# Reordering three waits in a two-layer streaming encoder step

## The chip, the cores and the metric

The kernel runs on one core of one Trainium2 chip, as one program. The metric is the device time of an execution in microseconds. An execution's profile has its own span, from the first to the last instruction, a little under its time.

## The reference

One inference step of two layers over 1074 columns: 16 meta tokens, 1024 prompt tokens, 32 sample tokens and 2 columns of padding, each with 1024 features.

```python
z = rmsnorm(x, norm_mix_g) @ w_in                 # split: c_q 768, c_kv 256, k_r 32, x_r 512, g_r 512
q = rmsnorm(c_q, q_norm_g) @ w_uq                 # 8 heads of 64 + 32 rotary
ckv, kpe = rmsnorm(c_kv, kv_norm_g), rope(k_r)
xc = causal_conv4(x_r); r, i = sigmoid(blockdiag(xc)), sigmoid(blockdiag(xc))
h = scan(a*h + sqrt(1-a^2)*(i*xc)); y = h * gelu(g_r)
k, v = ckv_keys @ w_ukv                           # K 64 and V 64 per head
o = softmax(mask(q k / sqrt(96))) v               # chunk-causal, chunks of 64
h = x + concat(rmsnorm(o), rmsnorm(y)) @ w_out
x = h + square(relu(rmsnorm(h) @ w_up)) @ w_down  # 4096 wide
```

After the second layer follows a last RMSNorm. All is float32.

## The kernel before

Activations lie transposed: 128 features on the partitions, the tokens along a row. Weights come in blocks of 128x1024, one DMA each from SyncE into `raw`. ScalarE rounds a block into `whi`, VectorE subtracts to get the remainder `wlo` (`split(b)` on either engine), and TensorE makes each product in three passes (high x high, high x low, low x high) over the k-steps, a pass being three matmuls of some 358 columns (`product`, L947 to L960). The results of one product fill three PSUM banks, banks 0 to 2 and 3 to 5 in turn (a slot); a product therefore waits (`take`) until the results of the product two before it have been read. Banks 6 and 7 take sums of squares and the first head's maxima.

There is no scheduler. Each engine's instructions stand in the order of its own function, and semaphores with counted values tie them together. A wait holds all that stands behind it on its engine. The places of the change are:

The start of a layer. In the first layer products 0 and 1 of the x_r columns are interleaved. In the second, product `U_XR[0]` is followed by `mix_sum` (L993), a product of a matrix of ones with `msq`, the sum of the squared inputs; its result goes into the root that scales every output of the input projection. VectorE builds `msq` by seven additions (`next_sq`, `next_sum`, L3098 to L3103), at the end of the first layer's `closing`, beside the last additions of the MLP (`d_sum`), the low parts of the next inputs (`next_low`) and the split of the first two weight blocks (`next_split`).

The maxima of the first head (`max_step(0, s)`, L1088). For each head the row maximum of the masked scores is needed as a shift for the exponentials. It is taken over 11 steps, `MAXES`. TensorE writes a step's scores into one of two banks, alternately (`max_bank`), and VectorE's `reduce_max(h, s)` takes the maxima of its parts; step s waits for the reduction of step s - 2, `w("mxred", h * NMX + s - 1)`. For head 0 the steps stand between the four K products (`B_UK`, three banks of 432 columns each) and the ten V tiles (six matmuls of 512 columns each, L1132 to L1145). `max_rows` (L1119) then transposes the maxima on TensorE, ScalarE copies them out (`shift_hi`, behind the copy of V tile 5), VectorE makes the low part (`shift_lo`), and SyncE and GpSimd write both into rows of the query tile (`qe`) by DMA (`few_shifts` for GpSimd); attention starts when all of them have landed. Behind reduction 3, VectorE also makes `kslot_lo`, a subtraction of 33x1296 with two inputs in SBUF, while GpSimd does three such subtractions (`low_parts`).

The output projection. Eight products of the LRU half (`U_OY`), then eight of the attention half (`U_OO`). VectorE adds the first eight to x (`add_y(i)`, an addition of one slot), normalises the last pair of heads (`divide(3)`, which waits until GpSimd's DMAs have spread the inverted sums of the softmax), and makes the low parts of the attention output (`o_low`). Product i of the LRU half waits for `add_y(i - 2)`. ScalarE's stream is the counterpart: high parts, squares, roots.

The MLP that follows takes about half of the time. It multiplies by blocks of two-level combinations of the weights (seven products in place of eight); its weight buffers are filled by DMAs that SyncE and GpSimd issue when the split of their last content is done.

Of the kernel before, what the change touches and what calls it, by code (L numbers as in the profile page):

```python
# [356 lines left out]
NMX = len(MAXES)  # L357
# [60 lines left out]
def trunk(nc, xT, wst, vec, fgain, ropeC, ropeS, ident_in, past_ckv, past_kpe, h0, conv0,  # L418
          yT, ckv_out, kpe_out, h_out, conv_out, x_scr, sum_scr):
    ctx = ExitStack()  # L420
    with ctx:
# [498 lines left out]
        def _(pe):  # L920
# [5 lines left out]
            for L in range(DEPTH):  # L926
# [20 lines left out]
                def product(dst, u, b, woff, rhs_h, rhs_l, ready=None):  # L947

                    w("w_lo", b + 2)
                    take(u)  # L950
                    n = len(rhs_h)
                    for k in range(n):
                        if ready:
                            ready(k)
                        for i, (a, c) in enumerate(PASSES):
                            wt = (whi if a == "h" else wlo)[b % 2][:, woff + 128 * k:woff + 128 * k + 128]
                            r = (rhs_h if c == "h" else rhs_l)[k]
                            for q in range(3):
                                mm = nc.tensor.matmul(dst(q), wt, r(q), start=(k == 0 and i == 0), stop=(k == n - 1 and i == 2))  # L959
                    mm.then_inc(S["mm"], 1)  # L960
# [32 lines left out]
                def mix_sum():  # L993

                    if L:
                        pe.wait_ge(S["sq_sum"], L * 7 + 7)
                        sum_of_squares(SUM_MIX, msq)
                    else:
                        w("sum_lo", SUM_MIX)
                        sum_of_parts(SUM_MIX, rs_r, msq_r)  # L1000
# [10 lines left out]
                if L == 0:  # L1011

                    for k, c in [(0, 0), (1, 0), (0, 1), (1, 1)] + [(k, c) for k in range(2, 8) for c in (0, 1)]:
                        dst = to_slot(U_XR[c])
                        for i, (a, b) in enumerate(PASSES):
                            if k == 0 and i == 0:
                                w("w_hi", B_XR[c] + 1)
                            if k == 0 and i == 2:
                                w("w_lo", B_XR[c] + 2)
                            if c == 0 and i == 0:  # L1020
                                w("xg_hi", k + 1)
                            if c == 0 and i == 1:
                                w("xg_lo", k + 1)
                            wt = (whi if a == "h" else wlo)[B_XR[c] % 2][:, 128 * k:128 * k + 128]
                            for q in range(3):
                                mm = nc.tensor.matmul(dst(q), wt, (XH if b == "h" else XL)[k](q), start=(k == 0 and i == 0), stop=(k == 7 and i == 2))  # L1026
                        if k == 7:
                            mm.then_inc(S["mm"], 1)
                    mix_sum()
                else:  # L1030
                    product(to_slot(U_XR[0]), U_XR[0], B_XR[0], 0, XH, XL, x_ready)
                    mix_sum()
                    product(to_slot(U_XR[1]), U_XR[1], B_XR[1], 0, XH, XL)

                XHL, XLL = [tok(t, LIVE) for t in xgh], [tok(t, LIVE) for t in xgl]

# [87 lines left out]
                for j in range(4):  # L1124
                    product(lambda q: ps[:, 3 * slot_of(U_K + j) + q, 0:KCH], U_K + j, B_UK, 256 * j,
                            [(lambda q, t=t: t[:, q * KCH:(q + 1) * KCH]) for t in ckvh],
                            [(lambda q, t=t: t[:, q * KCH:(q + 1) * KCH]) for t in ckvl])
                    if j >= 1:
                        max_step(0, 2 * j - 2)
                        max_step(0, 2 * j - 1)  # L1130
                w("w_lo", B_UV + 2)
                for t in range(10):  # L1132
                    if t < 3:
                        w("kf", 3)
                    else:
                        w("v_ev", t - 2)
                    c0 = VTILES[t]
                    for k in range(2):
                        for i, (a, c) in enumerate((("h", "h"), ("h", "l"), ("l", "h"))):
                            mm = nc.tensor.matmul(ps[:, 3 + t % 3, :], (ckvh if a == "h" else ckvl)[k][:, c0:c0 + P],  # L1140
                                                  (whi if c == "h" else wlo)[B_UV % 2][:, 512 * k:512 * k + 512],
                                                  start=(k == 0 and i == 0), stop=(k == 1 and i == 2))
                    mm.then_inc(S["mm"], 1)
                    if t + 6 < NMX:
                        max_step(0, t + 6)  # L1145
                    if t == 5:
                        max_rows(0)

                w("kf", 4)
# [992 lines left out]
        def _(dve):  # L2142
# [34 lines left out]
            for L in range(DEPTH):  # L2177
# [448 lines left out]
                o_low(2)  # L2626
                add_y(1)
                split(31)
                divide(3)
                add_y(2)  # L2630
                o_low(3)
                split(32)
                add_y(3)
                sum_lo(osq_r, osq, osqt_r, SUM_O)
                add_y(4)
                split(33)
# [417 lines left out]
                def closing():  # L3054

                    j = NPAIR - 1

                    def at(name, k):
                        dve.wait_ge(S[name], L * PER[name] + pairs(name, j) + k)

                    last_third_sum()
                    up_block_sum(NGROUP, 0, 2)
                    up_lo(j, 3)
                    up_lo(j, 4)
                    c_sum(at, 0)
                    up_lo(j, 5)
                    relu(at, 0, False)
                    up_lo(j, 6)
                    up_lo(j, 7)
                    c_sum(at, 1)  # L3070
                    relu(at, 1, False)
                    up_lo(j, 8)
                    f_low(at, 0)
                    c_sum(at, 2)
                    relu(at, 2, False)
                    f_low(at, 1)
                    up_lo(j, 9)
                    relu(at, 3, False)
                    f_low(at, 2)
                    up_lo(j, 10)  # L3080
                    d_sum(at, j, 0)
                    f_low(at, 3)
                    for n in range(1, 4 if L < DEPTH - 1 else 6):
                        d_sum(at, j, n)
                    if L < DEPTH - 1:

                        def next_low(m):

                            dve.wait_ge(S["xg_hi"], L * 8 + 8 + (m + 1))
                            at("d_add", DONE_AT[m])  # L3090
                            lo(xgl[m][:, :], x[m], xgh[m][:, :], "xg_lo", col(V_GNEXT + m))

                        def next_split(b):

                            dve.wait_ge(S["w_hi"], (L + 1) * B_MLP + b + 1)
                            V.tensor_tensor(wlo[b][:, :], raw[b][:, :], whi[b][:, :].bitcast(F32), ALU.subtract).then_inc(S["w_lo"], 1)

                        def next_sum(m):  # L3098

                            dve.wait_ge(S["sq"], L * 8 + 8 + m + 1)  # L3100
                            if m > 1:
                                dve.wait_ge(S["sq_sum"], L * 7 + 7 + m - 1)
                            V.tensor_tensor(msq[:, :], msq[:, :], next_sq[m][:, :], ALU.add).then_inc(S["sq_sum"], 1)  # L3103

                        for n in range(4, 16):
                            d_sum(at, j, n)
                            if n in (5, 7, 8, 10, 12, 14):
                                next_low((5, 7, 8, 10, 12, 14).index(n))
                            if n in (9, 13):
                                next_sum((n - 5) // 4)  # L3110
                            if n == 11:
                                next_split(0)
                        next_low(6)
                        next_sum(3)
                        next_low(7)
                        for m in (4, 5, 6, 7):
                            next_sum(m)
                        next_split(1)
                    else:
                        for n in range(6, 24):  # L3120
                            d_sum(at, j, n)
                            if n in (15, 17, 19, 20, 22):
                                end_scale(0, (15, 17, 19, 20, 22).index(n))
                        for m in range(5, 8):
                            end_scale(0, m)
                        for q in (1, 2):
                            for m in range(8):
                                end_scale(q, m)
# [343 lines left out]
```

## Time and profile before

| what | us |
|---|---|
| three timed runs | 2481.19, 2485.27, 2485.93 |
| median | 2485.27 |
| profiled execution, its own time | 2481.51 |
| its span | 2479.70 |

The timeline view lists instructions by start time, with neighbours of the same kind merged (x3 is three of them), their time together, and in brackets the idle time in front with what ended it, if there was any to speak of. TensorE's matmuls overlap in it: each lasts until its result is out, while the next one starts when its columns have been fed, so for TensorE it is the distance of the starts that counts. Its durations are modelled.

### The profile page before, as it was taken

The numbers are of one execution on the slowest core, as the hardware profiler recorded it, in microseconds if no ns is written. First come the engines' busy times: TensorE is split into PE (matmuls) and PEld (weight loads), VectorE is DVE, ScalarE is ACT, GpSimd is POOL, SyncE is SP. The second block draws the span as 40 slices with busy tenths as digits, with TensorE's granted clock in tenths as the row PEclk, the third lists the DMA queues.
The fourth block names the chain that finished last, engine by engine and source line by source line (L and its number), as shares of the span: only waits on it lengthen the run. The fifth ranks groups of instructions, "written<-read, shape, count | busy, mean of one in ns | idle before, by whom it ended". The sixth has DMA issues, their size and how long they took to land.

```text
span 2479.7 us, 43928 instructions
## 1 busy us (share of the span) xinstructions
PE 2458.4 (99%) x17424; PEld 2371.6 (96%) x17424; DVE 1802.2 (73%) x2778; ACT 1220.1 (49%) x2197; POOL 516.0 (21%) x478
## 2 busy tenths in 40 slices
PE   9999999999999999999999999999999999999998
PEld 9999977899999999999999999779999999999997
DVE  7678766579776777677676797674887766776676
ACT  5455355535554454454524653555355544554455
POOL 0024155200112211221201232541001112111222
PEclk9999999999999999999999999999999999999999
DMA  4122201213347635764731222012135467546655
GB/s 155 59 60 72 61 11 38 84 57 110 87 93 137 121 86 102 132 116 89 220 99 52 61 72 61 11 38 89 60 114 99 92 122 130 104 91 117 130 113 172
DMA packets 104537, 230.39 MB, mean 93 GB/s; under 512 B 14816, under 2 KB 17984, under 8 KB 104336
## 3 DMA queue, kind: packets, MB, share of 16 engines
q0 software_dynamic: 43648, 89.14, 20.9%
q1 hardware_dynamic: 60544, 138.42, 17.7%
q8 instruction: 139, 2.28, 0.4%
q14 instruction: 62, 0.51, 0.1%
q10 hardware_dynamic: 144, 0.04, 0.0%
HBM read 144.03 MB, written 81.18 MB: 91 GB/s over the span
## 4 chain that ended last, share of the span: by engine, by line
PE 91%; DVE 4%; DMA 2%; issue 2%; ACT 1%; POOL 0%; SPq 0%; DVEq 0%; ACTq 0%; POOLq 0%
PE ps L959 27%; PE ps L1304 23%; PE ps L1353 20%; PE ps L1168 5%; PE ps L1183 4%; PE ps L1445 2%; PE ps L1238 2%; PE ps L1115 2%; PE ps L1416 1%; DMA raw_all<-in_wst 1%; PE ps L1026 1%; PE ps L1140 1%; PE ps L1047 1%; DVE wlo L2809 1%; DVE raw_all L2941 0%
## 5 line engine op out<-in xcount | busy, mean ns | idle before, releaser
L1974 ACT ACTIVATE whi<-raw_all 128x512 fp32r<-128x512 f32 (+1 forms) x420 | 250.2, 600 | 348.2 <-DVE raw_all L2941 128.0
L2809 DVE TENSOR_TENSOR wlo<-raw_all,whi 128x512 fp32r<-128x512 f32 (+1 forms) x420 | 271.4, 652 | 174.6 <-ACT whi L1974 170.5
L3307 POOL DMA_DIRECT2D x_scratch<-stage x224 | 199.7, 942 | 845.9 <-DVE stage L2951 698.1
L2027 ACT ACTIVATE stage<-ps 128x536 f32<-128x536 f32 (+1 forms) x224 | 135.3, 610 | 110.0 <-PE ps L1353 104.6
L1497 ACT ACTIVATE whi<-raw_all 128x1024 fp32r<-128x1024 f32 (+3 forms) x72 | 66.7, 926 | 236.9 <-PE ps L959 234.4
L2951 DVE TENSOR_TENSOR stage<-stage,ps 128x536 f32<-128x536 f32 (+1 forms) x168 | 118.8, 707 | 85.8 <-PE ps L1353 84.8
L2519 DVE TENSOR_REDUCE mxp<-ps 64x1 f32<-64x64 f32 (+11 forms) x384 | 140.3, 372 | 55.0 <-PE ps L1115 48.4
L959 PE MATMUL ps<-xgh,whi 128*128 128x358 f32 (+1 forms) x720 | 157.3, 327 | 0.0
L959 PE MATMUL ps<-xgl,whi 128*128 128x358 f32 (+1 forms) x720 | 156.6, 325 | 0.0
L959 PE MATMUL ps<-xgh,wlo 128*128 128x358 f32 (+1 forms) x720 | 156.5, 325 | 0.0
L959 PEld LDWEIGHTS ps<-xgl,whi 128*128 128x128 f32 x720 | 124.0, 189 | 0.0
L959 PEld LDWEIGHTS ps<-xgh,whi 128*128 128x128 f32 x720 | 123.4, 189 | 0.5 <-issue 0.2
L959 PEld LDWEIGHTS ps<-xgh,wlo 128*128 128x128 f32 x720 | 123.3, 189 | 0.0
L2194 DVE TENSOR_TENSOR wlo<-raw_all,whi 128x1024 fp32r<-128x1024 f32 (+3 forms) x70 | 87.3, 1247 | 40.9 <-ACT whi L1497 40.5
L1168 PE MATMUL ps<-pn,v 128*65 128x320 f32 (+1 forms) x288 | 106.3, 452 | 0.0
L1755 ACT ACTIVATE pn<-ps 128x320 f32<-128x320 f32 (+1 forms) x144 | 65.4, 454 | 71.4 <-PE ps L1183 70.0
L2941 DVE TENSOR_TENSOR raw_all<-raw_all 128x256 f32<-128x256 f32 x224 | 90.4, 419 | 11.6 <-DMA raw_all<-in_wst 10.5
L1183 PE MATMUL ps<-qo,koh 128*128 128x320 f32 (+7 forms) x304 | 97.0, 400 | 0.0
L1183 PE MATMUL ps<-qe,keh 97*128 97x320 f32 (+7 forms) x304 | 95.7, 396 | 0.9 <-DMA qe<-mt 0.7
L1755 ACT ACTIVATE pd<-ps 16x64 f32<-16x64 f32 (+4 forms) x352 | 56.8, 224 | 55.5 <-PE ps L1183 55.2
L3292 POOL DMA_DIRECT2D raw_all<-in_wst x30 | 29.8, 993 | 254.8 <-DMA raw_all<-in_wst 254.8
L1183 PEld LDWEIGHTS ps<-qe,keh 97*128 97x128 f32 x304 | 54.6, 190 | 26.5 <-issue 7.4
(835 smaller groups left out, 7680.0 us busy)
## 6 DMA issues: line engine op xcount, KB each, us to landing
raw_all<-in_wst SPq DMA_DIRECT2D x232, 256.0 KB, 3.3
raw_all<-in_wst SPq DMA_DIRECT2D x80, 512.0 KB, 3.6
x_scratch<-stage POOLq DMA_DIRECT2D x112, 268.0 KB, 5.8
x_scratch<-stage POOLq DMA_DIRECT2D x112, 264.0 KB, 5.8
x_scratch<-xall POOLq DMA_DIRECT2D x24, 537.0 KB, 3.6
xall<-x_scratch SPq DMA_DIRECT2D x24, 537.0 KB, 9.4
xall<-in_xT SPq DMA_DIRECT2D x16, 537.0 KB, 7.4
raw_all<-in_wst POOLq DMA_DIRECT2D x30, 256.0 KB, 4.0
```

The costliest lines, as they stand in the source:

```text
L959: mm = nc.tensor.matmul(dst(q), wt, r(q), start=(k == 0 and i == 0), stop=(k == n - 1 and i == 2))
L1168: mm = nc.tensor.matmul(ps[0:65, bank, c0:c0 + n], v[:, v0:v0 + 65], p_tile(gk)[:, 0:n], start=(k in FIRST), stop=(k in LAST))
L1183: mm = nc.tensor.matmul(ps[:, gi % 3, 0:n], ks[e][0 if a == "h" else 1][rows, k0:k0 + P], qs[e][0 if c == "h" else 1][rows, q0:q0 + n], st ...
L1304: mm = nc.tensor.matmul(ps[:, 2 * slot_ + t, 0:HN], wt, rhs[:, t * HN:(t + 1) * HN], start=(opens and n == 0), stop=(n == 11), skip_group_ ...
L1353: mm = nc.tensor.matmul(ps[:, 2 * slot_ + t, 0:HN], ring(u, whi if a == "h" else wlo)[:, wc], fop[q, f + c][:, t * HN:(t + 1) * HN], start ...
L1755: ins = nc.scalar.activation(dst[r0:r1, c0:c1], src[r0:r1, c0:c1], ACT.Exp, scale=SM_SCALE)
L1974: nc.scalar.activation(dst, src, ACT.Copy).then_inc(S["u_hi"], 1)
L2027: nc.scalar.activation(quarters(stage_of(L, g, i, n)[:, 0:N2]), src, ACT.Copy, scale=-1.0 if row else 1.0).then_inc(S["x_copy"], 1)
L2519: ins = V.reduce_max(mxp[lo_:hi_, tile, part:part + 1], ps[lo_:hi_, max_bank(h, s), c0:c0 + n], AX_X)
L2809: V.tensor_tensor(dst, src, hi.bitcast(F32), ALU.subtract).then_inc(S["u_lo"], 1)
L2951: V.tensor_tensor(st, st, src, op).then_inc(S["x_add"], 1)
L3307: pool.dma_start(x_scr[2 * i + row, :, a:b], stage_of(L, g, i, n)[:, 0:b - a], accum_op=ALU.add).then_inc(S[done], 16)
```

## The change

Four edits in the order of instructions. The computation is the same, and so is the number of instructions of each engine.

1. On TensorE, in the second layer, `mix_sum` stands inside product `U_XR[1]`, ahead of its k-step 2, and not ahead of the whole product.
2. On VectorE, at the end of the first layer, `next_split(1)` (the low part of the weights of that product) stands ahead of the last four `next_sum`, not behind them.
3. On TensorE, head 0's steps stand in threes (0 to 2, 3 to 5, 6 to 8) behind K products 1 to 3, and steps 9 and 10 behind V tiles 0 and 1; before there were pairs, and one step behind each of V tiles 0 to 4. The transposition stands behind V tile 3, not 5. This holds for both layers.
4. On VectorE, `add_y(2)` stands ahead of `divide(3)`, and `add_y(3)` right behind it, ahead of `o_low(3)` and `split(32)`.

```diff
                     product(to_slot(U_XR[0]), U_XR[0], B_XR[0], 0, XH, XL, x_ready)
-                    mix_sum()
-                    product(to_slot(U_XR[1]), U_XR[1], B_XR[1], 0, XH, XL)
+                    product(to_slot(U_XR[1]), U_XR[1], B_XR[1], 0, XH, XL, lambda k: mix_sum() if k == 2 else None)
...
                     if j >= 1:
-                        max_step(0, 2 * j - 2)
-                        max_step(0, 2 * j - 1)
+                        for s in range(3 * j - 3, 3 * j):
+                            max_step(0, s)
...
-                    if t + 6 < NMX:
-                        max_step(0, t + 6)
-                    if t == 5:
+                    if t + 9 < NMX:
+                        max_step(0, t + 9)
+                    if t == 3:
                         max_rows(0)
...
                 add_y(1)
                 split(31)
+                add_y(2)
                 divide(3)
-                add_y(2)
+                add_y(3)
                 o_low(3)
                 split(32)
-                add_y(3)
                 sum_lo(osq_r, osq, osqt_r, SUM_O)
...
                         next_low(7)
+                        next_split(1)
                         for m in (4, 5, 6, 7):
                             next_sum(m)
-                        next_split(1)
```

TensorE's order of the first layer between K products 1 and 3, before. `keh` holds the first head's keys and `qe` its queries, and a row with them is a part of a step; the rows of L959 are the K product between the two pairs of steps.

```order
L1115 MATMUL ps<-keh,qe 128x144 [waits kslot_hi,k_hi,root,q_hi,qn_hi]
L1115 MATMUL ps<-keh,qe 128x272
L1115 MATMUL ps<-keh,qe 128x16
L1115 MATMUL ps<-keh,qe 128x400
L959 MATMUL ps<-ckvh_111,whi_51 128x432 [waits kf,w_lo]
...
L959 MATMUL ps<-ckvh_112,wlo_53 128x432 x3
L1115 MATMUL ps<-keh,qe 128x400 [waits mxred]
L1115 MATMUL ps<-keh,qe 128x128 [waits mxred]
L1115 MATMUL ps<-keh,qe 128x176
```

And of the changed kernel, in the same place.

```order
L1114 MATMUL ps<-keh,qe 128x144 [waits kslot_hi,k_hi,root,q_hi,qn_hi]
L1114 MATMUL ps<-keh,qe 128x272
L1114 MATMUL ps<-keh,qe 128x16
L1114 MATMUL ps<-keh,qe 128x400
L1114 MATMUL ps<-keh,qe 128x400 [waits mxred]
L959 MATMUL ps<-ckvh_111,whi_51 128x432 [waits kf,w_lo]
...
L1114 MATMUL ps<-keh,qe 128x128 [waits mxred]
L1114 MATMUL ps<-keh,qe 128x176
L1114 MATMUL ps<-keh,qe 128x512 [waits mxred]
L1114 MATMUL ps<-keh,qe 128x144 [waits mxred]
L1114 MATMUL ps<-keh,qe 128x272
```

Step 2 (400 columns, waiting for a reduction) now stands directly behind steps 0 and 1 and ahead of the K product, and the next group has steps 3, 4 and 5.

VectorE's order in the first layer's output projection, before. `o_150` is the last pair of heads, L2608 is `add_y`, and x_in7 and x_in0 name the additions with number 2 and 3.

```order
L2194 TENSOR_TENSOR wlo_53<-raw_all,whi_51 128x1024 [waits w_hi]
L2552 MEMSET o_150 128x2 [waits o_ev,inv_in]
L2553 TENSOR_TENSOR o_150<-o_150,rc 128x1072
L2608 TENSOR_TENSOR xall<-xall,ps 128x1074 [waits mm,x_in7]
L2224 SCALAR_TENSOR_TENSOR ol_166<-o_150,vecs,oh_162 128x1074 [waits o_sq,o_hi]
L2194 TENSOR_TENSOR wlo_52<-raw_all,whi_50 128x512 [waits w_hi]
L2608 TENSOR_TENSOR xall<-xall,ps 128x1074 [waits mm,x_in0]
```

And of the changed kernel, where each line number is one less.

```order
L2193 TENSOR_TENSOR wlo_53<-raw_all,whi_51 128x1024 [waits w_hi]
L2607 TENSOR_TENSOR xall<-xall,ps 128x1074 [waits mm,x_in7]
L2551 MEMSET o_150 128x2 [waits o_ev,inv_in]
L2552 TENSOR_TENSOR o_150<-o_150,rc 128x1072
L2607 TENSOR_TENSOR xall<-xall,ps 128x1074 [waits mm,x_in0]
L2223 SCALAR_TENSOR_TENSOR ol_166<-o_150,vecs,oh_162 128x1074 [waits o_sq,o_hi]
L2193 TENSOR_TENSOR wlo_52<-raw_all,whi_50 128x512 [waits w_hi]
```

Each of the two additions has moved up: the first past the division and its wait for `inv_in`, the second past a low part and a split.

## Rows read from the trace of the kernel before

**Rows 1.** The page, busy us and share of each engine.
```profile
PE 2458.4 (99%) x17424; PEld 2371.6 (96%) x17424; DVE 1802.2 (73%) x2778; ACT 1220.1 (49%) x2197; POOL 516.0 (21%) x478
```

**Rows 2.** Timeline, TensorE: start, us, instruction, count, idle before; first layer's output projection.
```profile
487.39 0.66 PE L959 MATMUL ps<-yh,wlo 128*128 128x358 f32 x3
489.05 0.72 PE L959 MATMUL ps<-yh,whi 128*128 128x358 f32 x3 [1.01 <-DVE xall L2608]
...
494.51 0.66 PE L959 MATMUL ps<-yh,wlo 128*128 128x358 f32 x3
495.18 0.73 PE L959 MATMUL ps<-yh,whi 128*128 128x358 f32 x3
```

**Rows 3.** Timeline, VectorE, the same stretch.
```profile
486.45 1.27 DVE L2553 TENSOR_TENSOR o<-o,rc 128x1072 f32<-128x1072 f32 x1 [7.65 <-issue]
...
487.64 1.26 DVE L2608 TENSOR_TENSOR xall<-xall,ps 128x1074 f32<-128x1074 f32 x1
```

**Rows 4.** The chain that ended last: start, us, what; second layer's output projection.
```profile
1698.43 34.87 PE ps L959 x216
```

**Rows 5.** Timeline, TensorE, start of the second layer.
```profile
1254.21 0.65 PE L959 MATMUL ps<-xgh,wlo 128*128 128x358 f32 x3
1255.46 2.14 PE L976 MATMUL ps<-msq,ones 128*128 128x512 f32 x6 [0.61 <-DVE msq L3103]
```

**Rows 6.** Timeline, VectorE and ScalarE, start of the second layer.
```profile
1249.99 5.41 DVE L3103 TENSOR_TENSOR msq<-msq,next_sq 128x1074 f32<-128x1074 f32 x4
1255.32 1.22 DVE L3096 TENSOR_TENSOR wlo<-raw_all,whi 128x1024 fp32r<-128x1024 f32 x1
...
1263.17 1.12 ACT L1559 ACTIVATE rs<-ps,eps 128x1024 f32<-128x1024 f32 x1
...
1266.93 1.28 DVE L2217 TENSOR_TENSOR t<-ps,rs 128x1074 f32<-128x1074 f32 x1 [0.95 <-ACT rs L1562]
```

**Rows 7.** Timeline, TensorE, first layer's K products and first steps.
```profile
283.80 0.70 PE L1115 MATMUL ps<-keh,qe 96*128 96x144 f32 x4
284.33 0.76 PE L959 MATMUL ps<-ckvh,whi 128*128 128x432 f32 x3
...
287.88 0.54 PE L1115 MATMUL ps<-keh,qe 96*128 96x400 f32 x3
```

**Rows 8.** Timeline in narrow windows, VectorE and GpSimd, first layer's reductions.
```profile
285.37 0.16 DVE L2519 TENSOR_REDUCE mxp<-ps 16x1 f32<-16x16 f32 x1
...
288.20 2.99 POOL L3227 TENSOR_TENSOR kel<-kf,keh 64x1296 fp32r<-64x1296 f32 x1
288.26 1.31 DVE L2519 TENSOR_REDUCE mxp<-ps 128x1 f32<-128x400 f32 x4 [2.07 <-PE ps L1115]
288.75 0.81 DVE L2519 TENSOR_REDUCE mxp<-ps 128x1 f32<-128x64 f32 x3
289.60 2.97 DVE L2222 TENSOR_TENSOR kel<-kpe,keh 33x1296 fp32r<-33x1296 f32 x1
292.60 0.69 DVE L2519 TENSOR_REDUCE mxp<-ps 128x1 f32<-128x512 f32 x1
```

**Rows 9.** Timeline, ScalarE and TensorE, second layer's start of attention.
```profile
1534.21 0.60 ACT L1736 ACTIVATE v<-ps 128x512 f32<-128x512 f32 x1 [0.98 <-PE ps L1140]
...
1542.23 0.55 PE L1183 MATMUL ps<-qe,keh 97*128 97x336 f32 x2 [0.73 <-DMA qe<-mt]
```

**Rows 10.** Timeline, GpSimd and TensorE, first layer's start of attention.
```profile
304.65 0.53 POOL L3254 DMA_DIRECT2D qe<-mt  x1
...
307.36 0.40 PE L1140 MATMUL ps<-whi,ckvl 128*128 128x512 f32 x1
```

**Rows 11.** DMA issues from 303 to 309 us: count, KB, us to landing.
```profile
qe<-mt POOLq DMA_DIRECT2D x1, 0.2 KB, 2.8
```

**Rows 12.** Waits: who waited for whom, us in total, times, longest.
```profile
PEld ps L1353 <- ACT whi L1974: 3.0, 4, 1.2
...
PEld ps L1304 <- ACT whi L1974: 1.2, 2, 0.6
```

## The prediction

> **What bounds the kernel now.** I read the busy shares first. TensorE is busy for 2458.4 us, 99% of the span [rows 1], so its stream of matmuls is the path to the end, and an edit counts only through a gap that it closes or opens in that stream. So I then read the timeline of TensorE for gaps at the three places that the change touches, and the timelines of the engines that end those gaps.
>
> The first place is the output projection of the first layer. Passes of three matmuls follow each other every 0.49 us, but between 487.39 and 489.05 lie 1.66 us, and the releaser is VectorE's addition at L2608 [rows 2]. VectorE ran that addition at 487.64, right behind the last division, which had sat 7.65 us idle and began at 486.45 [rows 3]. The second layer has no such gap: its chain has 216 matmuls of L959 in one piece of 34.87 us, which is six products [rows 4]. The second place is the start of the second layer: between the last pass of the first product (1254.21) and the sum of squares (1255.46) lie 1.25 us instead of 0.49, ended by VectorE's last running sum [rows 5]. The third is the first head's maxima, between the four K products and the ten V tiles. There is no gap there: four matmuls (steps 0 and 1) at 283.80, the next K product at 284.33, the next pair of steps at 287.88 [rows 7]. The steps alternate between two banks of PSUM, and a step waits until the maxima of the step two before it have been taken. In pairs that wait is always long over.
>
> **The additions around the last division.** Nothing is added; `add_y(2)` and `add_y(3)` move ahead. The product that `add_y(2)` needs ended at about 482 (two of the 5.9 us products before 494), so it runs in the 7.65 us of idle time, the division still starts at 486.45 when its data have landed, and `add_y(3)` follows it. The TensorE gap of 1.66 - 0.49 = 1.17 us closes. The next product started at 495.18, 0.67 us behind the pass at 494.51 [rows 2], which is 0.18 over the spacing, since `add_y(3)` had just ended; that closes too. Each of these two restarts also had a first pass of about 0.56 us instead of 0.49, another 0.14 in all. Gain 1.17 + 0.18 + 0.14 = 1.5 us in layer 0, nothing in layer 1. The fourth part of `o_low` now stands behind `add_y(3)`, but its readers are the attention half of the projection, four products away, which hides it; uncovered it would cost one addition, 1.26 us [rows 3].
>
> **The sum of squares inside the product, and the split ahead of the sums.** In place of waiting at 1254.21 + 0.49 = 1254.70, TensorE goes on with the second product. That needs the split of its weights, which ran at 1255.32 [rows 6]; moved ahead of the four running sums it runs from 1249.99 to about 1251.2. The four sums (5.41 us) then end at 1251.2 + 5.41 = 1256.6 instead of 1255.40. TensorE does two of eight k-steps first, 6 passes x 0.49 = 2.96 us, and comes to the sum at 1257.66, 1.0 us after it is ready. So the 0.76 us of waiting goes and nothing takes its place; without that 1.0 us of slack a new wait would stand there. What is later is the sum itself, by about 2 us (1257.7 for 1255.5). ScalarE read its result only at 1263.17 [rows 6], so that is hidden too, and the first evacuation at 1266.93 to 1268.2 is even unmoved in time for the third product, at 1268.5. SyncE's next weight load and, behind it, the loads of the second layer's vectors wait for the moved split, so they are issued some 5 us earlier; nothing near them waits for a DMA in their place. Gain 0.8 us. Bounds: 0 if the sum waited as long inside the product as before it, 0.8 as a whole.
>
> **The maxima in threes.** This is the part that costs. The third step of each group uses the bank of the group's first step, so TensorE, which runs in order, now stands still until VectorE has reduced the first step, while the next K product waits behind it. From matmul to reduction I take a tail of 0.21 us: steps at 287.88 with 400 columns (0.17 us at the spacing of the matmuls) release the reduction at 288.26 [rows 7, 8]. From VectorE's end to the matmul I take 0.15 (488.90 to 489.05) [rows 2, 3].
> Group one: the last reduction of step 0 ends at 285.37 + 0.16 = 285.53 [rows 8], step 2 starts at 285.68, where the stream was free at 284.33. Wait 1.35 us.
> Group two: step 3 has 304 columns (0.13 us), tail 0.21, its three reductions 0.81 [rows 8], restart 0.15, together 1.30; steps 3 and 4 fill 0.36 of it. Wait 0.94 us.
> Group three: step 6 has 512 columns (0.23), tail 0.21, reduction 0.69 [rows 8], restart 0.15, together 1.28; steps 6 and 7 fill 0.46. Wait 0.82 us.
> That is 3.11 us per layer. Bounds: at least the reductions themselves less what the group computes meanwhile (about 0.85 x 3 = 2.5), at most 3.5 if each restart also costs a slow first pass.
> Then the start of attention. It waits for rows that go from the transposed maxima through ScalarE, VectorE and DMAs. The transposition now comes two tiles earlier, but ScalarE takes the rows in its order, behind the copies of V tiles 4 and 5, so they still hang on the V tiles. In layer 1 the copy of V tile 4 starts at 1534.21 and attention at 1542.23, 8.0 us later, released by a DMA after 0.73 us of idle time [rows 9]. Seen from V tile 4 this chain keeps its length, but step 10 (0.23 us) and the transposition (0.12) now stand ahead of V tile 4 and not behind it. So layer 1 pays 3.11 + 0.35 = 3.46 us. In layer 0 attention was not waiting, but only just: the DMA issued by GpSimd at 304.65 took 2.8 us and landed at 307.45, with the last V matmul at 307.36 [rows 10, 11]. With 3.46 more it lands at 310.91, and with the 0.25 us that layer 1 shows from landing to matmul, attention starts at 311.16 instead of 307.65: 3.5 us. Together 7.0 us.
>
> One instruction on VectorE decides whether group three is longer. The subtraction at L2222 behind step 3 took 2.97 us [rows 8], and GpSimd's at L3227 ran until 288.20 + 2.99 = 291.19 [rows 8]. It now starts 1.0 us later, at about 290.6, still inside that GpSimd instruction; I take its end as unmoved (292.57), so step 4's and 5's maxima are done at 294.3 as before, in time for step 7 at 294.7.
> The Trainium skill (GPSIMD Engine Reference, section 1, Specifications) says that GpSimd shares its SBUF interfaces with VectorE and that they contend when a VectorE instruction has two SBUF inputs. By that reading the 2.97 us are 1.6 us of waiting and 1.37 of work, the end at 292.57 stays, and the sum is as above; were 2.97 us its own length, the rival below with +0.8 us would hold.
>
> **Sum.** 7.0 - 1.5 - 0.8 = +4.7 us. Against the profiled execution of 2481.51 us that gives 2486.2. The three timed runs have 2481.19, 2485.27 and 2485.93, so two of four executions lie 4 us above the other two; the profiled one is 3.8 below the median. The mean of the four is 2483.5, and I predict 2483.5 + 4.7 = 2488.2 us, a slowdown of 0.19%, almost exactly at the 0.2% that a measurement of this kernel can tell from no change.
>
> **Rivals.**
> (a) The subtraction takes 2.97 us wherever it starts. It ends at 293.6, step 5's maxima at about 295.3, step 7 waits until 295.45 and step 8 until 296.2 instead of 295.8: +0.4 us per layer, +5.5 us, 2489.0 us. For it: only one instance per layer was measured. Against: both ended 1.37 us after GpSimd did in this kernel's timeline.
> (b) The shift rows no longer hang on V tile 4 (ScalarE gets at them earlier). Then attention starts with the V tiles' end: layer 0 pays 3.1, layer 1 3.1 - 0.7 (its DMA wait [rows 9]), total 5.5 - 2.3 = +3.2 us, 2486.7 us. Against: the order of ScalarE's stream is unchanged.
> (c) Not slower: the MLP's waits swallow the delay. TensorE's weight loads of L1353 and L1304 wait 3.0 and 1.2 us for ScalarE's rounded weights [rows 12], which hang on DMAs from HBM. If those DMAs kept their times, up to 4.2 of the 4.7 us would vanish: +0.5 us, 2484.0 us, and not slower at all as far as one can measure; it decides when the transfers are issued without regard to TensorE. Against: SyncE issues each only when a buffer was freed by work behind TensorE, so they move with the stream.
> (d) The gain in the projection fails because the division's data land earlier than 486.45 in other executions, so that the old order had no gap: 1.5 us less gain, +6.2 us, 2489.7 us.
>
> **Numbers.** Forecast 0.55, (a) 0.14, (b) 0.12, (c) 0.10, (d) 0.09. The range goes from the faster pair with (b), 2481.2 + 3, to the slower pair with (d), 2485.9 + 6.2: 2484 to 2492. Since the forecast lies at the edge of 0.2%, it gives slower 0.20 and same 0.35; (a) 0.08 and 0.06; (d) 0.06 and 0.03; (b) 0.01 and 0.11; (c) same 0.06, faster 0.04. In sum faster 0.04, same 0.61, slower 0.35.
>
> **What would show it.** In the profile after: no gap around 482 to 495 in the first layer's projection; the sum of squares at the second layer's start without idle time in front of it; inside each of the three groups of steps of both layers, TensorE idle 1.35, 0.94 and 0.82 us behind VectorE's reductions; attention released by a DMA in both layers. I would be wrong if the groups showed no gap, if the attention phase started less than 3 us later relative to the first step, or if the span of the MLP shrank by as much as was lost before it.

## The result, and the profile after

| kernel | median us | lowest to highest | runs |
|---|---|---|---|
| before | 2483.72 | 2480.77 to 2487.89 | 22 |
| changed | 2487.14 | 2483.36 to 2495.23 | 22 |

The ratio is 1.0014, with a 95% interval of 1.0008 to 1.0021: 3.4 us slower, where 4.7 were forecast (2488.2 us). The interval leaves out a ratio of 1, so the kernel is slower, but by an amount that lies almost wholly below the 0.2% which the prediction took as the least that a measurement can tell.

The profiled executions have spans of 2479.7 and 2487.6 us. That is 7.9 us, more than twice what the medians say, so the first thing to learn from the two traces is which differences belong to the change. Timeline of TensorE after, first layer's steps of the first head (columns as in the rows before the prediction):

```profile
283.31 0.70 PE L1114 MATMUL ps<-keh,qe 96*128 96x144 f32 x4
285.10 0.45 PE L1114 MATMUL ps<-keh,qe 96*128 96x400 f32 x1 [1.10 <-DVE mxp L2518]
...
288.95 0.61 PE L1114 MATMUL ps<-keh,qe 96*128 96x128 f32 x3
290.23 0.50 PE L1114 MATMUL ps<-keh,qe 96*128 96x144 f32 x2 [0.67 <-DVE mxp L2518]
...
294.11 0.63 PE L1114 MATMUL ps<-keh,qe 96*128 96x512 f32 x2
295.29 0.46 PE L1114 MATMUL ps<-keh,qe 96*128 96x400 f32 x2 [0.55 <-DVE mxp L2518]
```

Where [rows 7] had none, each group now has a gap in front of its third step, ended by VectorE's reduction. The bracket counts idle time from the modelled end of a matmul; counted from where the stream could have gone on (start of the matmul before, plus its columns at 0.455 ns each, the spacing of the V tiles' matmuls: 0.233 us for 512 columns) the three are 1.34, 0.85 and 0.71 us in both layers. An expectation below gives them as 1.36, 0.87 and 0.73; it counts 0.4167 ns for a column, which is less than the spacing that the trace shows.

VectorE and GpSimd after, at the second group:

```profile
287.69 2.96 POOL L3226 TENSOR_TENSOR kel<-kf,keh 64x1296 fp32r<-64x1296 f32 x1
...
289.34 0.83 DVE L2518 TENSOR_REDUCE mxp<-ps 128x1 f32<-128x64 f32 x3 [3.04 <-PE ps L1114]
290.20 1.82 DVE L2221 TENSOR_TENSOR kel<-kpe,keh 33x1296 fp32r<-33x1296 f32 x1
292.05 1.71 DVE L2518 TENSOR_REDUCE mxp<-ps 128x1 f32<-128x512 f32 x5
```

The subtraction that took 2.97 us in [rows 8] takes 1.82 here. Its end, 292.02, is 1.37 us behind GpSimd's end at 287.69 + 2.96 = 290.65; before the change it was 1.38 behind (292.57 and 291.19).

TensorE after, the last V tile and the start of attention in the first layer, and the same in the second; they answer to [rows 10] and [rows 9]:

```profile
309.89 0.40 PE L1139 MATMUL ps<-whi,ckvl 128*128 128x512 f32 x1
310.58 0.55 PE L1182 MATMUL ps<-qe,keh 97*128 97x336 f32 x2 [0.30 <-DMA qe<-mt]
...
1546.74 0.40 PE L1139 MATMUL ps<-whi,ckvl 128*128 128x512 f32 x1
1548.22 0.55 PE L1182 MATMUL ps<-qe,keh 97*128 97x336 f32 x2 [1.08 <-DMA qe<-mt]
```

Both layers now wait for the DMA with the shift rows. The last places are the chain of waits after, which answers to [rows 4] and to the gap in [rows 2], and the weights' waits in the MLP:

```profile
466.93 35.28 PE ps L959 x216
...
1246.31 14.98 PE ps L959 x90
1261.30 1.87 PE ps L976 x6
1263.17 112.44 PE ps L959 x684
```

The first layer's projection is now one piece of 216 matmuls, as the second layer's was. The sum of squares (L976) stands between 90 and 684 matmuls, 90 being ten k-steps of nine, with no wait on either side. VectorE's last running sum ended at 1260.03 and TensorE came to the sum at 1261.14.

Waits of TensorE's weight loads after (engine, line, waited for: us in total, times, longest), answering to [rows 12]:

```profile
PEld ps L1352 <- ACT whi L1973: 6.6, 4, 2.3
...
PEld ps L1352 <- issue: 1.7, 6, 0.5
...
PEld ps L1303 <- ACT whi L1973: 1.2, 2, 0.6
```

These are MLP waits that the change does not touch, 9.5 us in this execution. The same three groups were 3.0, 1.8 and 1.2 us before, 6.0 in all; the last experiment shows that they differ between executions of one kernel.

To put the terms apart, I take distances between the starts of two matmuls in one timeline; they are free of what an execution spends elsewhere.

| stretch | before | after | difference |
|---|---|---|---|
| first step to attention, layer 0 (283.31 to 310.58 after) | 23.86 | 27.28 | +3.42 |
| attention to the LRU half of the projection, layer 0 | 156.46 | 155.95 | -0.51 |
| LRU half, layer 0 | 49.94 | 48.45 | -1.49 |
| start of layer 1 to its K products | 267.63 | 266.73 | -0.90 |
| first step to attention, layer 1 | 24.71 | 28.11 | +3.40 |
| attention to the LRU half, layer 1 | 155.80 | 155.83 | +0.03 |

They add up to +3.95 us. The MLP phases, counted from the attention half of the projection on, add 4.44 in this pair of profiles (the 9.5 for 6.0 us above are most of it), and the time ahead of the first K product is 0.49 shorter; that makes the 7.9 us between the spans.

### The profile page after: what moved, and what is told of

Same layout as the page of the kernel before. It is cut to its first block, busy times and chain, and to the rows that moved or that the text cites. A ratio compares the mean times of both kernels' runs of the same rounds, so it can differ in the third digit from the quotient of the medians.

```text
span 2487.6 us, 43928 instructions
## 1 busy us (share of the span) xinstructions
PE 2458.7 (99%) x17424; PEld 2370.6 (95%) x17424; DVE 1800.8 (72%) x2778; ACT 1221.1 (49%) x2197; POOL 516.2 (21%) x478
## 4 chain that ended last, share of the span: by engine, by line
PE 92%; DVE 3%; DMA 2%; issue 1%; ACT 1%; POOL 0%; SPq 0%; DVEq 0%; ACTq 0%; POOLq 0%
PE ps L959 28%; PE ps L1303 23%; PE ps L1352 20%; PE ps L1167 5%; PE ps L1182 4%; PE ps L1444 3%; PE ps L1237 2%; PE ps L1114 2%; DMA raw_all<-in_wst 1%; PE ps L1415 1%; PE ps L1026 1%; DVE mxp L2518 1%; PE ps L1046 1%; DVE wlo L2808 1%; PE ps L1139 1%
## 5 line engine op out<-in xcount | busy, mean ns | idle before, releaser
L959 PE MATMUL ps<-xgh,whi 128*128 128x358 f32 (+1 forms) x720 | 157.3, 327 | 0.0
L959 PE MATMUL ps<-xgl,whi 128*128 128x358 f32 (+1 forms) x720 | 156.6, 325 | 0.0
L959 PE MATMUL ps<-xgh,wlo 128*128 128x358 f32 (+1 forms) x720 | 156.5, 325 | 0.0
L959 PEld LDWEIGHTS ps<-xgl,whi 128*128 128x128 f32 x720 | 124.0, 189 | 0.0
L959 PEld LDWEIGHTS ps<-xgh,whi 128*128 128x128 f32 x720 | 123.4, 189 | 0.5 <-issue 0.2
L959 PEld LDWEIGHTS ps<-xgh,wlo 128*128 128x128 f32 x720 | 123.3, 189 | 0.0
```

## Experiments

The theory is the one on record: the threes cost some 7 us, the additions give 1.5 and the sum inside the product 0.8. Ratios are to the kernel before, run on the same chip.

**threes_alone**: the kernel before with the third edit alone.

```diff
-                        max_step(0, 2 * j - 2)
-                        max_step(0, 2 * j - 1)
+                        for s in range(3 * j - 3, 3 * j):
+                            max_step(0, s)
```

> The kernel before with only the maxima in threes and the transposition behind V tile 3. Theory (the third steps wait for VectorE): from the first step to the start of attention 27.3 us in layer 0 and 28.1 in layer 1, where before had 23.86 and 24.71, and nothing else changed by design; the time is 6.8 us above before, 1.0027. Rival (part of these waits is given back later, in attention or the MLP, which is why the whole change measured +3.4 us and not the sum of 4.7): the same two stretches, but the time only 4 to 5 us above before.

Measured: 2491.21 us, ratio 1.0027 (1.0017 to 1.0036). First step to attention 27.27 and 28.06 us; the first layer's stretch behind it is 156.00 us for 156.46, the others are as before within 0.2 us. The four stretches from the first steps to the projection are together 6.3 us longer. TensorE's first group:

```profile
283.44 0.70 PE L1115 MATMUL ps<-keh,qe 96*128 96x144 f32 x4
285.23 0.45 PE L1115 MATMUL ps<-keh,qe 96*128 96x400 f32 x1 [1.10 <-DVE mxp L2519]
```

The same gap of 1.10 us by the bracket as in the changed kernel: the threes make it by themselves and cost 6.7 us by the time (4.2 to 8.9). The rival expected 4 to 5 us; the interval does not exclude that, but the stretches do: of the 6.8 us up to the starts of attention they give back 0.5.

**without_threes**: the other three edits; the diff is against the changed kernel.

```diff
-                        for s in range(3 * j - 3, 3 * j):
-                            max_step(0, s)
+                        max_step(0, 2 * j - 2)
+                        max_step(0, 2 * j - 1)
...
-                    if t + 9 < NMX:
-                        max_step(0, t + 9)
-                    if t == 3:
+                    if t + 6 < NMX:
+                        max_step(0, t + 6)
+                    if t == 5:
                         max_rows(0)
```

> The change without its maxima in threes: the sum inside the product, the split ahead of the sums and the two additions stay. Theory: the projection of layer 0 takes 48.45 us from its first product to the attention half (49.94 before), the input projection of layer 1 0.9 us less than before, the stretch from first step to attention as before (23.9 and 24.7); the time is 2.4 us below before, 0.9990. Rival (the two gains are swallowed by the next wait): both stretches shorter, but the time as before within 1 us.

Measured: 2481.93 us, ratio 0.9989 (0.9979 to 1.0000). The LRU half takes 48.45 us, the second layer's start to K 266.73, first step to attention 23.78 and 24.73. Together with threes_alone this splits the result: -2.7 + 6.7 = +4.0 us from two separate kernels, for the +3.4 measured on the kernel with all the edits.

**additions_only**: the fourth edit alone.

```diff
+                add_y(2)
                 divide(3)
-                add_y(2)
+                add_y(3)
                 o_low(3)
                 split(32)
-                add_y(3)
```

> The kernel before with only the two additions ahead of the last division and split. Theory: 48.45 us instead of 49.94 from the first product of the projection to its attention half in layer 0, 47.89 as before in layer 1, all else as before: 1.5 us below before, 0.9994, too little for the clock. Rival (the division's data come at another time in another execution): the gap in layer 0 was of one execution, and the stretch differs by less than 1 us.

Measured: 2481.12 us, ratio 0.9992 (0.9982 to 1.0001), so by time alone it is not told from no change; the profile tells it. The LRU half takes 48.45 us in the first layer (49.94 before) and 47.89 in the second, as before. The chain of waits and VectorE's timeline of this kernel:

```profile
463.77 35.28 PE ps L959 x216
```

```profile
485.71 1.27 DVE L2553 TENSOR_TENSOR o<-o,rc 128x1072 f32<-128x1072 f32 x1 [2.91 <-issue]
...
487.76 1.27 DVE L2608 TENSOR_TENSOR xall<-xall,ps 128x1074 f32<-128x1074 f32 x1 [0.78 <-PE ps L959]
```

The division still waits for its data (2.91 us idle, where 7.65 stood in [rows 3]), and the addition behind it now waits for TensorE (0.78) and not the other way round. Every profile with the old order shows 49.85 to 49.97 us for this stretch, every one with the new order 48.45, so the gap is no accident of one execution.

**sum_inside_only**: the first edit without the second.

```diff
-                    mix_sum()
-                    product(to_slot(U_XR[1]), U_XR[1], B_XR[1], 0, XH, XL)
+                    product(to_slot(U_XR[1]), U_XR[1], B_XR[1], 0, XH, XL, lambda k: mix_sum() if k == 2 else None)
```

> The kernel before with only the sum of squares moved inside the second product; the split of that product's weights stays behind the running sums. Theory (the split is what makes the move pay): the second product cannot start at 12.0 us behind the first one's start but waits until 13.9, when the split is done, 1.9 us of idle time in place of 0.76, so the layer's input projection is 1.1 us longer than before. Rival (the sum was the only thing in the way): the same 0.8 us gain as in the whole change.

Measured: 2484.90 us, ratio 1.0014 (1.0004 to 1.0024), start of layer 1 to K 268.72 us, 1.1 more than before. In time that is +1.0 to +6.0 us, which just holds the 1.1; the size is read from the profile. TensorE and VectorE:

```profile
1253.55 0.65 PE L959 MATMUL ps<-xgh,wlo 128*128 128x358 f32 x3
1255.94 0.76 PE L959 MATMUL ps<-xgh,whi 128*128 128x358 f32 x3 [1.75 <-DVE wlo L3095]
```

```profile
1252.10 2.66 DVE L3102 TENSOR_TENSOR msq<-msq,next_sq 128x1074 f32<-128x1074 f32 x2
1254.67 1.22 DVE L3095 TENSOR_TENSOR wlo<-raw_all,whi 128x1024 fp32r<-128x1024 f32 x1
```

The wait for the sum is gone, and a longer one stands in its place: the second product needs the split, which VectorE reaches only behind the sums. The starts lie 2.39 us apart in place of 0.49, a gap of 1.90. So the move of one call on TensorE costs 1.1 us by itself and gives 0.9 with the split ahead. The two edits are one.

**third_step_in_product**: the other three edits, with the third step of each group inside the next K product, steps 8 to 10 behind V tiles 0 to 2, the rows copied earlier and VectorE's subtraction `kslot_lo` two reductions later. It asks whether the threes can be had without their wait. The diff is against the kernel before.

```diff
-                        max_step(0, 2 * j - 2)
-                        max_step(0, 2 * j - 1)
+                        max_step(0, 3 * j - 3)
+                        max_step(0, 3 * j - 2)
...
-                            [(lambda q, t=t: t[:, q * KCH:(q + 1) * KCH]) for t in ckvl])
+                            [(lambda q, t=t: t[:, q * KCH:(q + 1) * KCH]) for t in ckvl],
+                            (lambda k, j=j: max_step(0, 3 * j - 4) if k == 1 else None) if j >= 2 else None)
...
-                    if t + 6 < NMX:
-                        max_step(0, t + 6)
-                    if t == 5:
+                    if t + 8 < NMX:
+                        max_step(0, t + 8)
+                    if t == 3:
                         max_rows(0)
...
+                    if t == 3:
+                        shift_hi(0)
                     if t == 4:
                         nc.scalar.activation(spw[:, 4:8], spw[:, 0:4], ACT.Exp, scale=-1.0)
-                    if t == 5:
-                        shift_hi(0)
...
-                    if s == 3:
+                    if s == 5:
                         kslot_lo(0, 0, KW)
```

> As the kernel without threes, but step 2 and step 5 stand inside the next K product ahead of its second k-step, steps 8 to 10 behind V tiles 0 to 2, the transposition behind V tile 3; VectorE makes the subtraction of L2222 behind reduction 5 and not 3, and ScalarE takes the rows of the maxima right behind the copy of V tile 3. Theory (only the wait of a third step costs, not its number, and the shift rows come by their order on ScalarE): no idle time of TensorE among the steps, attention starts with the end of the V tiles, 23.8 us after the first step in both layers; 3.3 us below before, 0.9987. Rival (the bank's reduction or the moved subtraction is late anyway): idle time of 0.5 us or more in front of a step, or attention still waiting in layer 1, and the time as the kernel without threes.

Measured: 2481.80 us, ratio 0.9991 (0.9981 to 1.0001), 2.3 us below before where 3.3 were expected, and by time not told from without_threes (0.9989). First step to attention 23.87 and 23.83 us. TensorE at the third step of the first group:

```profile
285.30 0.75 PE L959 MATMUL ps<-ckvh,wlo 128*128 128x432 f32 x3
285.89 0.35 PE L1114 MATMUL ps<-keh,qe 96*128 96x400 f32 x1
286.08 0.76 PE L959 MATMUL ps<-ckvh,whi 128*128 128x432 f32 x3
```

There is no idle time in front of the step, so the wait is that of the bank's reduction and not of three steps as such: with one of the K product's two k-steps between, it is over before TensorE comes. The second layer's attention starts 0.9 us earlier than before, but the stretch behind it is 156.26 us for 155.80. What takes half of it back is seen in TensorE's weight loads a little behind the start:

```profile
1542.07 0.19 PEld L1114 LDWEIGHTS ps<-koh,qo 128*128 128x128 f32 x1 [0.42 <-DVE mxp L2518]
```

**threes_rows_early**: the changed kernel, with the copy of the shift rows ahead of a load of ScalarE's table for the exponential. It is the test of rival (b).

```diff
                     if t == 4:
+                        shift_hi(0)
                         nc.scalar.activation(spw[:, 4:8], spw[:, 0:4], ACT.Exp, scale=-1.0)
-                    if t == 5:
-                        shift_hi(0)
```

> The whole change, but ScalarE takes the rows of the maxima behind the copy of V tile 4, ahead of the table load, and not behind V tile 5. Theory (the late start of attention beyond the three waits is ScalarE's order): attention starts with the end of the V tiles, in layer 0 0.4 us earlier than in the change (26.9 us after the first step for 27.28), in layer 1 1.2 us earlier (26.9 for 28.11); the three waits stay at 1.36, 0.87 and 0.73 us. Rival (it hangs on another of attention's waits): both stretches as in the change.

Measured: 2486.48 us, ratio 1.0008 (0.9997 to 1.0018). The three waits stand (1.34, 0.85 and 0.71 us), attention starts with the end of the V tiles in both layers, and first step to attention is 26.86 and 26.81 us, 0.42 and 1.30 less than in the changed kernel. ScalarE's timeline of this kernel, and then the changed kernel's:

```profile
303.66 0.60 ACT L1735 ACTIVATE v<-ps 128x512 f32<-128x512 f32 x1 [0.54 <-PE ps L1139]
304.15 0.25 ACT L1722 ACTIVATE mt<-ps 10x128 fp32r<-10x128 f32 x1
304.42 1.28 ACT L1741 ACT_TABLE_LOAD   x1
```

```profile
304.03 1.28 ACT L1741 ACT_TABLE_LOAD   x1
305.33 0.21 ACT L1741 ACTIVATE spw<-spw 128x4 f32<-128x4 f32 x1
305.44 0.58 ACT L1735 ACTIVATE v<-ps 128x512 f32<-128x512 f32 x1
305.92 0.25 ACT L1722 ACTIVATE mt<-ps 10x128 fp32r<-10x128 f32 x1
```

What the rows waited for in the changed kernel was the table load of 1.28 us and the copy behind it. But the stretches behind are 156.58 and 156.28 us in place of 155.95 and 155.83, so some 0.6 and 0.45 us come back. The same wait shows here:

```profile
1547.10 0.19 PEld L1114 LDWEIGHTS ps<-koh,qo 128*128 128x128 f32 x1 [0.42 <-DVE mxp L2516]
```

and in the first layer of the kernel before, with VectorE's part of it:

```profile
307.80 0.36 DVE L2506 CAST koh<-kf 64x400 fp32r<-64x400 f32 x1 [3.12 <-PE ps L1140]
...
310.40 1.68 DVE L2519 TENSOR_REDUCE mxp<-ps 128x1 f32<-128x80 f32 x6
311.73 0.19 PEld L1115 LDWEIGHTS ps<-koh,qo 128*128 128x128 f32 x1 [0.42 <-DVE mxp L2519]
```

VectorE starts on the next head's keys (`koh`) when TensorE has ended the V tiles, not when attention begins, and a step of that head waits for its reduction 3.9 us later. Whoever starts attention right behind the V tiles meets this wait; whoever starts it 0.4 us late, as the changed kernel does in the first layer (27.28 for 26.86 us), has less than 0.1 us of it.

**table_load_late**: without_threes, with the table load behind the copy of the rows.

```diff
-                    if t == 4:
-
-                        nc.scalar.activation(spw[:, 4:8], spw[:, 0:4], ACT.Exp, scale=-1.0)
                     if t == 5:
                         shift_hi(0)
+                    if t == 6:
+                        nc.scalar.activation(spw[:, 4:8], spw[:, 0:4], ACT.Exp, scale=-1.0)
```

> As the kernel without threes, but ScalarE loads the table of the exponential behind V tile 6 and takes the rows of the maxima ahead of it. Theory (in layer 1 the start of attention hangs on ScalarE's queue): its rows are taken 0.4 us earlier, the stretch to attention in layer 1 is 24.3 us instead of 24.7, in layer 0 23.8; the time 0.4 us below the kernel without threes, which only the profile can tell. Rival (it hangs on the DMAs or GpSimd alone): 24.7 us again.

Measured: 2480.78 us, ratio 0.9987 (0.9977 to 0.9996), the lowest of all and the only one whose interval lies below 1. The first step to attention takes 23.80 and 24.25 us; in the second layer attention now waits 0.28 us by the bracket where [rows 9] has 0.73:

```profile
1538.33 0.55 PE L1182 MATMUL ps<-qe,keh 97*128 97x336 f32 x2 [0.28 <-DMA qe<-mt]
```

Its distance from without_threes (0.9989) is within both intervals, so that this last move helps is shown in the profile and not in the time.

**before_again**: the kernel before, unchanged, profiled once more.

> The kernel before, unchanged, for one more profile. The whole change's profile has 10.3 us of waits of TensorE in the MLP where the profile of before has 5.9. Theory (these differ by execution, whatever the order elsewhere): the waits in the MLP of this execution differ by over 1 us from 5.9, while the stretches of the three edits repeat within 0.2 us. Rival (they belong to the kernel): 5.9 us again within 0.5.

Measured: one run of 2483.19 us, span 2481.4. The stretches of the table are 23.82, 156.37, 49.97, 267.59, 24.57 and 155.82 us, at most 0.14 from the first profile. The waits of the weight loads:

```profile
PEld ps L1353 <- ACT whi L1974: 4.2, 4, 1.4
...
PEld ps L1353 <- issue: 3.0, 8, 0.5
...
PEld ps L1304 <- ACT whi L1974: 1.2, 2, 0.6
```

That is 8.4 us for the same instructions that waited 6.0 in the first profile. table_load_late, which is faster, shows 3.2 and 2.5 in the two groups of its L1352. So these waits differ between executions of one kernel. From the attention half of the projection on, the MLP phases take 1462.6 and 1465.0 us in the two profiles of before and 1467.0 in that of the changed kernel; whether the last 2.0 us are chance or belong to the change, one profile of it does not show.

## Why the prediction came out as it did

The sign, the main term and the order of the terms were right; the sum was 1.3 us too high, and the interval of the measurement (+2.0 to +5.2 us) holds it.

**The additions** gave 1.49 us for 1.5, all in the first layer. Rival (d), no gap in other executions, is refuted by four profiles with the gap in the old order and six without it in the new one.

**The sum of squares and the split** gave 0.90 for 0.8, and the slack ahead of the sum was 1.1 us for 1.0. That the bound of "nothing" belongs to the move without the split, and even lies below nothing, the prediction did not say; sum_inside_only put it at +1.1 us.

**The threes.** The waits were forecast as 1.35, 0.94 and 0.82 us and are 1.34, 0.85 and 0.71, 2.90 in place of 3.11 a layer. The tail of 0.21 us was right (0.20 in the second and third group). The restart was not: the reductions end at 285.04, 290.17 and 295.23 and TensorE starts 0.05 us behind each, where I took 0.15 from the projection. In the third group that is the whole difference. In the second, steps 3 and 4 also take 0.43 us of the stream and not 0.36. The first wait came out exact by luck: its restart was 0.10 us too long, but the moment from which it was counted, 284.33, was 0.08 too late, since the 400 columns of step 1 start at 284.07 and at the stream's spacing are fed by 284.25. The start of attention moved by 3.42 and 3.40 us for 3.5 and 3.46. In the first layer 3.00 of it is the later end of the V tiles (26.86 us in threes_rows_early for 23.86) and 0.42 the wait for the rows, so the mechanism was right there too.

**The step that was mis-sized** is the last of that part, "attention starts at 311.16 instead of 307.65: 3.5 us". The start is 3.42 later, but the price in the first layer is 0.51 us less, since TensorE no longer comes ahead of VectorE's reduction. TensorE before, from the first attention matmul to the one behind the waiting step, and the latter after:

```profile
307.65 0.55 PE L1183 MATMUL ps<-qe,keh 97*128 97x336 f32 x2
...
312.01 0.38 PE L1168 MATMUL ps<-pd,v 128*65 128x128 f32 x2
```

```profile
314.54 0.38 PE L1167 MATMUL ps<-pd,v 128*65 128x128 f32 x2
```

The distance was 4.36 us and is 314.54 - 310.58 = 3.96: 0.40 of the 0.51 us; the other 0.11 I did not trace. I had stopped at the start of a phase and had not asked what waits stood behind it. With 2.9 for 3.5 there, and 3.4 in the second layer, the threes cost 6.3 us by the profile in place of 7.0, and the whole +3.95. The 0.6 us between that and the medians' 3.4 the interval does not resolve.

**Rival (a)**, the subtraction of 2.97 us wherever it starts, is refuted: 1.82 us in the first layer. The second layer before, and after:

```profile
1521.74 2.98 POOL L3227 TENSOR_TENSOR kel<-kf,keh 64x1296 fp32r<-64x1296 f32 x1
...
1523.32 2.76 DVE L2222 TENSOR_TENSOR kel<-kpe,keh 33x1296 fp32r<-33x1296 f32 x1
```

```profile
1524.80 2.95 POOL L3226 TENSOR_TENSOR kel<-kf,keh 64x1296 fp32r<-64x1296 f32 x1
...
1526.99 2.12 DVE L2221 TENSOR_TENSOR kel<-kpe,keh 33x1296 fp32r<-33x1296 f32 x1
```

VectorE's end lies 1.36 us behind GpSimd's in both (1526.08 and 1524.72, 1529.11 and 1527.75). third_step_in_product, which has the subtraction behind reduction 5 and so behind GpSimd's (ended at 290.97), shows it alone:

```profile
291.66 1.50 DVE L2221 TENSOR_TENSOR kel<-kpe,keh 33x1296 fp32r<-33x1296 f32 x1
```

It takes 1.50 us there and 1.51 in the second layer, so 2.97 us is not its own length. The sentence of the Trainium skill that the prediction weighed (GPSIMD Engine Reference, section 1, Specifications) says that the two engines contend for shared SBUF interfaces. The four instances agree with it, and their common end 1.37 us behind GpSimd's shows the contention as a wait.

**Rival (b)**, rows that do not hang on V tile 4, did not happen, and threes_rows_early made it happen: attention starts 1.72 us earlier in the two layers together, but 1.08 us of that comes back behind the starts. The ratio is 1.0008 (0.9997 to 1.0018) for 1.0014, which the intervals do not tell apart.

**Rival (c)**, MLP waits that swallow the delay, is refuted for this size: threes_alone kept its 6.7 us in the time, and the MLP's waits were larger after, not smaller. That they vary by 2.4 us between two executions of one kernel is why neither profile's span could decide it.

**The base was wrong in its reason.** I read three timed runs and a profiled one as two pairs 4 us apart. The 22 runs lie spread from 2480.77 to 2487.89 without two levels, and the mean of four that I used, 2483.5, came close to their median (2483.72) by luck. The range of 2484 to 2492 was built on the same two pairs.

## What to carry to other kernels

Before a step is put where it reuses a buffer that an earlier step of its own group filled, add the reader's time to the tail and the restart and see how much of other work stands between: three steps on two banks stall by what the reader takes, and the same three with half a product between the second and the third do not. A wait that is taken away in one engine's order pays only with the next thing that this order needs, so the two moves are judged together. When a phase starts late or early, follow it to its first internal wait before its whole shift is put into the sum, and when two spans are compared, first take out the waits that two executions of the same kernel differ by.

## What the hardware showed that I had not expected

- A VectorE subtraction of 33x1296 with two SBUF inputs, begun while GpSimd ran one of 64x1296, ended 1.36 to 1.38 us behind GpSimd's end in all four instances that I read, whether it had begun 1.59, 1.40, 0.76 or 0.45 us ahead of that end, and so in the fourteen others of the runs' profiles. Begun after GpSimd's subtraction, it took 1.50 and 1.51 us. What it did beside GpSimd thus shortened its own 1.5 us by 0.14 at most, however long the two ran together: it waits, and does not run at half rate.
- ScalarE's table load, 1.28 us each time, lay on the path of a few hundred bytes that a whole phase waited for.
- Two profiles of one kernel agree to 0.14 us in stretches of 24 to 268 us outside the MLP, and differ by 2.4 us in the MLP's waits for weights alone.
